# The router of a mixture-of-experts encoder on unscaled rows, and the prompt's list of rows made ahead of the sample's

## Chip, cores and metric

One core of a Trainium2 chip runs the whole kernel. The metric is the device time of one execution in microseconds. Three executions of the kernel before took 2691.74, 2692.01 and 2695.96 us, a median of 2692.01 us.

## What is computed

One layer of a bidirectional encoder is applied to two request groups with the same weights: 1024 tokens of a prompt and 256 of a sample, of 1024 columns. The change lies between the output projection and the first expert:

```python
x = x + concat(yA, yB) @ w_out
h = rms_norm(x, ffn_norm_w)                 # x * rsqrt(mean(x*x) + eps) * w
aff = softmax(h @ w_router)                 # 16 experts
gates, idx = top_k(aff.T, cap)              # each expert takes 128 prompt rows, 32 sample rows
for e in range(16):
    xe = h[idx[e]]
    ye = (silu(xe @ wg[e]) * (xe @ wu[e])) @ wd[e] * gates[e]
    out[idx[e]] += ye
x = x + out
```

The prompt and the sample are routed apart: the threshold of one doesn't depend on tokens of the other.

## The kernel before

Everything is a hand-written program for five queues: TensorE (`pe`), VectorE (`dve`), ScalarE (`act`), GpSimd (`pool`) and the DMA queue of SyncE (`sp`). Each queue runs its instructions in the order written, and the queues meet at semaphores. Float32 products are made of a rounded part (`fp32r`, names with `_h`, lines 734) and two bfloat16 cross products with what the rounding left (`_l`, lines 739 and 740).

**Output projection, tiles t = 0 to 9** of 128 tokens, 0 to 7 the prompt's, 8 and 9 the sample's. `wo_half(t, c)` makes 512 columns: eight rounded products, then sixteen cross products. Two halves lie in one PSUM tile `S[:, t % 2]`. Between them TensorE turns the normed rows of tile t-1 (`h2t`, line 728), turns that tile's router values (`aff`, line 1011), makes the router's partial products in four groups of 32 rows of the PSUM bank G (`router_parts`, line 991), turns the next tile's `yt`, and adds up the four groups (`router`, line 999). The last tile has no tile behind it whose products would cover it: `router(9)` takes sixteen wide instructions (line 1003).

**What VectorE does per tile.** It adds the residual (`x2t`, line 1879), forms the softmax of the tile before (lines 1886 to 1891), runs one or more rounds of the ranking, scales the rows by their rstd and the norm's weight (`h2t`, line 1902), copies the turned rows out of PSUM (`h2T`, line 1909), copies the turned router values to the work tile WK (line 1830), and forms the low parts of the next tile (`yT_l`, line 1824). ScalarE squares `x2t` for the norm (line 1439), GpSimd forms the rstd (lines 2133, 2135) and stores `x2t` (line 2307) and `h2t` (line 2309) to DRAM.

**Ranking.** An expert's 128 greatest of 1024 are found on VectorE in rounds: `MAX8` takes the eight greatest of a row, `MATCH_REPLACE8` takes them out (`best_eight`, lines 1837, 1839). Part 0 (tiles 0 to 3) and part 1 (tiles 4 to 7) take 16 rounds each, on 48 partitions; `merge` (lines 1845 to 1855) merges the halves of a part. The tables `ROUNDS_AHEAD` and `ROUNDS_BEHIND` say at which tile which rounds run, ahead of or behind the middle of VectorE's work. The last four rounds run after the last tile and on 80 partitions, the sample's among them (line 1927).

**Lists.** The threshold is turned by TensorE (line 1031) and compared with `aff` (`chosen`, line 1939); TensorE counts the ranks of the chosen rows (line 1036); VectorE forms places and one-hot rows (`oh` for the prompt, `ohs` for the sample, lines 1944 to 1959); TensorE multiplies them with row numbers and gates (lines 1061, 1064); VectorE adds the parts to indices (`index_sum`, lines 1971 to 1981). GpSimd splits `aff` into three bfloat16 parts for this (`gate_parts`, lines 2291 to 2299), and gathers the rows: `xe`, 128 prompt rows of 4 KB (line 2326), and `xsm`, two gathers of 128 pieces of 512 bytes, the sample's (line 2329).

**First expert.** TensorE turns `xe` and `xsm` (lines 1073, 1075), ScalarE rounds them to X (lines 1464, 1466), VectorE subtracts (lines 1992, 1995), GpSimd converts to bfloat16 (`Xb`, line 2346). Before that VectorE splits weight pieces 0 and 1 (`p_lows`, line 1986). Then 16 experts of 34 weight pieces follow; SyncE loads weights into four stages and waits for the split of a stage's last piece (line 701).

The lines on which the order at the end hangs:

```python
for r in range(r0, r1):                                  # 1835, best_eight
best_eight(1, 80, 12, 16)                                # 1927
onehots(1)                                               # 1999
index_sum(1)
dve.wait_ge(gather_sent, 1)
p_lows(0)
p_lows(1)
```

## Time and profile before

| What | Value |
|---|---|
| median of three executions | 2692.01 us |
| span of the profiled execution, which is its own time here | 2693.8 us |
| TensorE busy | 2606.6 us, 97% |
| VectorE, ScalarE, GpSimd busy | 1963.9, 1692.7, 1108.9 us |
| mean granted TensorE clock | 0.988 of full |
| output projection, all ten tiles | 615.6 to 751.0 us |
| from its last product to the first expert's first product | 751.0 to 793.4 us |
| sixteen experts and the final norm | 793.4 to 2693.8 us |
| GpSimd's constants of the lists, in tile 1 | 646.5 to 654.7 us |
| last index sum of the first expert ends | 781.03 us |

The page gives busy time and share for each engine, then the span in 40 slices; a slice is 67 us, so that the 42 us between the projection and the first expert show as one slice in which TensorE and its clock fall to 6 tenths. The timeline and the tables by stretch show what lies within it. The profile gives no time of its execution outside its span, so the span stands for it; it lies 1.8 us above the median.

### The profile page before, as it was taken

The numbers are of one execution on the slowest core, as the hardware profiler recorded it, in microseconds if no ns is written. First come the engines' busy times: TensorE is split into PE (matmuls) and PEld (weight loads), VectorE is DVE, ScalarE is ACT, GpSimd is POOL, SyncE is SP. The second block draws the span as 40 slices with busy tenths as digits, with TensorE's granted clock in tenths as the row PEclk, the third lists the DMA queues.
The fourth block names the chain that finished last, engine by engine and source line by source line (L and its number), as shares of the span: only waits on it lengthen the run. The fifth ranks groups of instructions, "written<-read, shape, count | busy, mean of one in ns | idle before, by whom it ended". The sixth has DMA issues, their size and how long they took to land. (4 is left out here: it accounts for less than half of the span.)

```text
span 2693.8 us, 53857 instructions
## 1 busy us (share of the span) xinstructions
PE 2606.6 (97%) x22588; PEld 2372.4 (88%) x22588; DVE 1963.9 (73%) x2361; ACT 1692.7 (63%) x2527; POOL 1108.9 (41%) x781
## 2 busy tenths in 40 slices
PE   7999999989959999999999999999999999999997
PEld 6666776665549999999999999999999999999997
DVE  6233256674668788888878888787878878788787
ACT  4366345562127676676767677676766767677675
POOL 2224201134125364452736346263644627354354
PEclk9999999999969999999999999999999999999998
DMA  7311312124557898979889897988988798898887
GB/s 188 76 46 32 74 37 44 36 85 150 168 199 274 314 313 297 330 256 342 293 319 315 292 333 258 340 294 314 322 293 322 269 330 304 311 323 289 317 299 285
DMA packets 365898, 652.18 MB, mean 242 GB/s; under 512 B 26599, under 2 KB 94055, under 8 KB 365623
## 3 DMA queue, kind: packets, MB, share of 16 engines
q1 hardware_dynamic: 349483, 605.63, 64.5%
q0 software_dynamic: 16176, 43.12, 6.3%
q8 instruction: 180, 2.95, 0.5%
q14 instruction: 59, 0.48, 0.1%
HBM read 612.81 MB, written 36.94 MB: 241 GB/s over the span
## 5 line engine op out<-in xcount | busy, mean ns | idle before, releaser
L1986 DVE TENSOR_TENSOR wl<-stg,wh 128x2048 bf16<-128x2048 f32 (+1 forms) x544 | 1241.0, 2289 | 256.6 <-ACT wh L1476 251.8
L1476 ACT ACTIVATE wh<-stg 128x2048 fp32r<-128x2048 f32 (+1 forms) x544 | 1010.9, 1861 | 196.2 <-PE S L1104 71.4
L2379 POOL TENSOR_TENSOR hx<-hh,hx 128x320 fp32r<-128x320 f32 x176 | 385.6, 2191 | 805.9 <-ACT hx L1529 805.6
L1101 PE MATMUL S<-X,wh 128*128 128x320 f32 x3760 | 591.0, 312 | 1.3 <-DVE X L1995 1.3
L1101 PEld LDWEIGHTS S<-X,wh 128*128 128x128 f32 x3760 | 557.1, 189 | 1.7 <-DVE X L1995 1.7
L1147 PE MATMUL S<-hx,wh 128*128 128x320 f32 x1892 | 312.6, 313 | 0.5 <-DVE yTs L2034 0.5
L1101 PE MATMUL OG<-X,wh 128*128 128x320 f32 x1872 | 298.2, 311 | 1.2 <-DVE gg L2016 1.2
L1104 PE MATMUL S<-Xb,wl 128*128 128x160 bf16 x3760 | 290.1, 233 | 0.0
L1147 PEld LDWEIGHTS S<-hx,wh 128*128 128x128 f32 x1892 | 280.8, 188 | 0.9 <-issue 0.6
L1101 PEld LDWEIGHTS OG<-X,wh 128*128 128x128 f32 x1872 | 277.4, 188 | 1.6 <-issue 1.4
L1104 PEld LDWEIGHTS S<-Xb,wl 128*128 128x128 bf16 x3760 | 258.9, 98 | 12.0
L2381 POOL CAST hb<-hx 128x320 bf16<-128x320 f32 x176 | 208.5, 1185 | 0.0
L1529 ACT ACTIVATE hx<-hh 128x320 fp32r<-128x320 f32 x176 | 83.1, 472 | 176.6 <-DVE hh L2023 176.6
L2208 POOL TENSOR_TENSOR ca<-lsum,half 128x20 f32<-128x20 f32 (+3 forms) x10 | 24.2, 2418 | 374.0 <-ACT o_all L1354 236.6
L1104 PE MATMUL S<-hb,wl 128*128 128x160 bf16 x1892 | 158.8, 233 | 0.0
L1147 PE MATMUL OG<-hx,wh 128*128 128x320 f32 x924 | 158.2, 313 | 0.2 <-DVE gg L2016 0.2
L1319 ACT ACTIVATE E<-E,nmax 128x1024 f32<-128x1024 f32 (+1 forms) x80 | 81.8, 1023 | 107.7 <-DVE nmax L1698 107.7
L1104 PE MATMUL OG<-Xb,wl 128*128 128x160 bf16 x1872 | 149.2, 233 | 0.0
L1104 PEld LDWEIGHTS S<-hb,wl 128*128 128x128 bf16 x1892 | 132.1, 98 | 8.1
L1147 PEld LDWEIGHTS OG<-hx,wh 128*128 128x128 f32 x924 | 138.6, 188 | 0.6 <-DVE gg L2016 0.6
L1104 PEld LDWEIGHTS OG<-Xb,wl 128*128 128x128 bf16 x1872 | 129.7, 98 | 6.0
L740 PE MATMUL OG<-hT_h,wkq_l 128*128 128x512 bf16 (+1 forms) x384 | 129.3, 350 | 0.0
(316 smaller groups left out, 3803.5 us busy)
## 6 DMA issues: line engine op xcount, KB each, us to landing
stg<-in_w_gate_dram SPq DMA_DIRECT2D x80, 2048.0 KB
stg<-in_w_up_dram SPq DMA_DIRECT2D x80, 2048.0 KB
stg<-in_w_down_dram SPq DMA_DIRECT2D x64, 2048.0 KB
stg<-in_w_down_dram SPq DMA_DIRECT2D x32, 1536.0 KB
stg<-in_w_gate_dram SPq DMA_DIRECT2D x16, 1024.0 KB
stg<-in_w_up_dram SPq DMA_DIRECT2D x16, 1024.0 KB
w_st<-in_w_in_dram SPq DMA_DIRECT2D x20, 512.0 KB, 4.0
yt<-mixed SPq DMA_DIRECT2D x10, 512.0 KB, 5.4
```

The source lines that it names most:

```text
L740: mm = pe.matmul(out, lhs_l(k), tops(rhs_h(k)), start=False, stop=(k == KT - 1))
L1101: pe.matmul(out, w, x, start=first, stop=False, skip_group_check=True)
L1104: return pe.matmul(out[:, 0:CT], w, x, start=False, stop=last, skip_group_check=True)
L1147: mm = pe.matmul(down_bank(e, d), whk[:, f, c * P:(c + 1) * P], hx[:, f0 + f, :], start=(f0 + f == 0), stop=(last and f0 + f == FT - 1), s ...
L1319: act.activation(e, e, ACT.Exp, scale=-1.0, bias=nmax[:, col:col + 1], accum_out=lsum[:, j % 2, t, hf:hf + 1]).then_inc(exp_done, 1)
L1476: act.activation(piece_conv(wh, g), piece_stage(g), ACT.Copy).then_inc(rounded, 1)
L1529: act.activation(hx[:, j - 1:j + 1, 0:CT], hh[:, :, :], ACT.Copy).then_inc(hidden_hi, 1)
L1986: dve.tensor_tensor(piece_conv(wl, g), piece_stage(g), piece_conv(wh, g).bitcast(F32), ALU.subtract).then_inc(split, 1)
L2208: own(pool.tensor_tensor(a, ls, minus_one, ALU.pow))
L2379: pool.tensor_tensor(hx[:, f, CT:2 * CT], hh[:, :, :], hx[:, f, 0:CT].bitcast(F32), ALU.subtract).then_inc(hidden_ready, 1)
L2381: pool.tensor_copy(hb[:, f, :], hx[:, f, 0:CT].bitcast(F32)).then_inc(hidden_b, 1)
```

## The change

The router's weight is multiplied once with the norm's weight, and the router runs on the unscaled rows `x2t`; the rstd is multiplied onto the logits. TensorE turns `x2t` in the midst of the next tile's products. The last tile takes the four groups too. ScalarE copies the turned rows and scales `h2t`, and GpSimd multiplies the norm's weight on and stores it. The rounds of the ranking are placed anew, the sample's four rounds run on its own 16 partitions after the prompt's threshold, and thresholds, ranks, one-hots, indices and gathers of the first expert are made for the prompt first, then for the sample.

```diff
-ROUNDS_AHEAD = {6: (0, 5, 6), 7: (0, 11, 12), 10: (1, 5, 6)}
-ROUNDS_BEHIND = {5: (0, 0, 5), 6: (0, 6, 11), 7: (0, 12, 16), 9: (1, 0, 5), 10: (1, 6, 11), 11: (1, 11, 12)}
+ROUNDS_AHEAD = {5: (0, 0, 8), 6: (0, 9, 16), 9: (1, 0, 8), 10: (1, 10, 16)}
+ROUNDS_BEHIND = {5: (0, 8, 9), 9: (1, 8, 10)}
...
+                sp.dma_start(fwT[:, :], ffn_norm_w[0].rearrange("(k p) -> p k", p=P)).then_inc(wrt_in, 16)
...
+            def wo_tile(t):
...
+                    highs(S[:, t % 2, cols], y_h(t), o_h(cols), range(KT))
+                    crosses(S[:, t % 2, cols], y_h(t), y_l(t), o_h(cols), o_l(cols), range(4))
+                    rows_turn(t - 1)
+                    crosses(S[:, t % 2, cols], y_h(t), y_l(t), o_h(cols), o_l(cols), range(4, KT))
+                    router_parts(t - 1)
+                cols = slice(512, 1024)
+                highs(S[:, t % 2, cols], y_h(t), o_h(cols), range(KT))
+                if t >= 1:
+                    router(t - 1)
+                if t + 1 < TT:
+                    y_turn(t + 1)
+                crosses(S[:, t % 2, cols], y_h(t), y_l(t), o_h(cols), o_l(cols), range(KT)).then_inc(mixed_ready, 1)
+                if t >= 1:
+                    aff_turn(t - 1)
+
+            def rows_turn(t):
+
+                pe.wait_ge(x2_ready, t + 1)
+                for c in range(2):
+                    turn(wo_fill["h", t] + c, [x2t[:, b * P:(b + 1) * P] for b in range(4 * c, 4 * c + 4)])
...
+            for t in range(TT):
+                wo_tile(t)
+            rows_turn(TT - 1)
+            router_parts(TT - 1)
+            router(TT - 1)
+            aff_turn(TT - 1)
...
+            for u in range(TT - 1):
+                x2_square(u)
+                x2_copies(u)
+                h2_scale(u)
+                parts_copy(u)
+                logit_exp(u)
+                if u + 2 < TT:
+                    y_round(u + 2)
+            x2_copies(TT - 1)
+            x2_square(TT - 1)
+            parts_copy(TT - 1)
+            h2_scale(TT - 1)
+            logit_exp(TT - 1)
...
+            def h2_scale(u):
+                act.wait_ge(rs2_ready, u + 1)
+                if u >= 1:
+                    act.wait_ge(h2_stored, 16 * u)
+                act.activation(h2t[:, :], x2t[:, :], ACT.Copy, scale=rsx[:, TT + u:TT + u + 1]).then_inc(h2_scaled, 1)
...
+            dve.wait_ge(wrt_in, 48)
+            dve.tensor_tensor(wrt[:, :, :], wrt[:, :, :], fwT[:, :].unsqueeze(2).to_broadcast([P, KT, NE]),
+                              ALU.mult).then_inc(wr_ready, 1)
...
+                own(dve.tensor_scalar(lz[:, v % 2, :], G[:, 0:NE], rsx[:, TT + v:TT + v + 1], None, ALU.mult))
...
+            merge(1)
...
+            dve.tensor_copy(least[:, :], cutoff[:, 0:1].to_broadcast([NE, P])).then_inc(cutoff_ready, 1)
+            affT_copy(TT - 1)
+            dve.wait_ge(cutoff_ps, 1)
+            choose(0, TPR, S[:, 0, 0:NE])
+            dve.wait_ge(affT_ready, TT)
+            best_eight(1, slice(64, 80), 0, 4)
+            dve.tensor_copy(least_s[:, :], ranked[64:80, 1, 31:32].to_broadcast([NE, P])).then_inc(cutoff_ready, 1)
...
+            place(0, TPR, ranks)
+            dve.wait_ge(cutoff_ps, 2)
+            choose(TPR, TT, S[:, 1, 0:NE])
...
+            row_onehots(1).then_inc(first_oh, 1)
+            dve.wait_ge(pos_ps, 2)
+            dve.wait_ge(chosen_ready, 2)
+            place(TPR, TT, ranks_s)
+            dve.wait_ge(h2_stored, 16 * TT)
+            piece_onehots(1)
...
-            onehots(1)
-            index_sum(1)
-            dve.wait_ge(gather_sent, 1)
+            dve.wait_ge(first_ps, 1)
+            row_sum(1).then_inc(first_idx, 1)
+            dve.wait_ge(idx_ps, 1)
+            piece_sum(1)
...
             p_lows(0)
             p_lows(1)
-            for q in range(4):
-                x_lows(q + 1, q, q)
             p_lows(2)
             onehots(2)
...
-                pool.wait_ge(h2_ready, t + 1)
+                pool.wait_ge(h2_scaled, t + 1)
+                if t == 0:
+                    pool.wait_ge(wrt_in, 48)
+                own(pool.tensor_tensor(h2t[:, :], h2t[:, :], fwb[:, :], ALU.mult))
+                own.wait()
                 pool.dma_start(octet_of(hn_d, t), h2t[:, :]).then_inc(h2_stored, 16)
...
+            pool.wait_ge(first_idx, 1)
+            stand()
+            gather_rows(1)
+            pool.wait_ge(idx_ready, 1)
+            stand()
+            gather_pieces(1)
```

TensorE waits for `Xb` only ahead of the first low products of an expert (`x_b`, `first_b_s`), no longer ahead of its first rounded ones.

TensorE in one tile of the projection, before: the second half's eight rounded products come after the turned rows and router values; of the runs of cross products (lines 739 and 740) the first two rows stand.

```order
L740 MATMUL S<-wo_h,yT_l 128x512
L728 MATMUL PT<-identf,h2t 128x128 x8
L1011 MATMUL OG<-identf,aff 16x128
L734 MATMUL S<-wo_h,yT_h 128x512 x8
L991 MATMUL OG<-h2T,wrt 16x128 x8
L728 MATMUL PT<-identf,yt_127 128x128 x8
L739 MATMUL S<-wo_l,yT_h 128x512
```

The same place of the change:

```order
L753 MATMUL S<-wo_h,yT_l 128x512
L741 MATMUL PT<-identf,x2t 128x128 x8
L752 MATMUL S<-wo_l,yT_h 128x512
...
L753 MATMUL S<-wo_h,yT_l 128x512
L1029 MATMUL OG<-h2T,wrt 16x128 x8
L747 MATMUL S<-wo_h,yT_h 128x512 x8
L1036 MATMUL OG<-sum_groups,part_logits 128x16
L741 MATMUL PT<-identf,yt_127 128x128 x8
L752 MATMUL S<-wo_l,yT_h 128x512
```

The turned rows moved forward into the first half's cross products, the router's sum from the end of the tile to the middle of its second half, and the turned router values (line 1042) behind the tile.

VectorE from the last tile's softmax to the places, before (`ranked` and WK are the ranking's tiles, `least` the threshold spread over 128 columns):

```order
L1891 TENSOR_SCALAR aff<-eg,rl_118 128x16
...
L1830 COPY WK<-OG 16x128
L1837 MAX ranked<-WK 80x8
L1839 MATCH_REPLACE WK<-ranked,WK 80x256
...
L1934 COPY least<-cutoff 16x128
L1939 TENSOR_TENSOR chosen<-aff,S 128x128 x2
L1939 TENSOR_TENSOR chosen<-aff,S 128x32 x2
L1944 SCALAR_TENSOR_TENSOR places<-chosen,S 128x320
```

and in the change:

```order
L2015 COPY least<-cutoff 16x128
L1911 COPY WK<-OG 16x128
L1999 TENSOR_TENSOR chosen<-aff,S 128x128 x2
L1918 MAX ranked<-WK 16x8
L1920 MATCH_REPLACE WK<-ranked,WK 16x256
...
L2021 COPY least_s<-ranked 16x128
L2004 SCALAR_TENSOR_TENSOR places<-chosen,S 128x2x128
L2007 TENSOR_TENSOR posm<-places 128x8x16
L1999 TENSOR_TENSOR chosen<-aff,S 128x32 x2
L2032 TENSOR_TENSOR oh<-iotaS,posm 128x1024
L2004 SCALAR_TENSOR_TENSOR places<-chosen,S 128x2x32
```

Four rounds moved from ahead of the prompt's threshold to behind it; they stand ahead of the prompt's places and one-hot rows still.

VectorE around the first expert's rows, before (`wl` are the low parts of the weights, X the rows):

```order
L1981 TENSOR_REDUCE gate<-PT 128x1
L1986 TENSOR_TENSOR wl<-stg,wh 128x2048 x2
L1992 TENSOR_TENSOR X<-PT,X 128x4x32
L1995 TENSOR_TENSOR X<-PT,X 128x2x128 x2
L1992 TENSOR_TENSOR X<-OG,X 128x4x32
L1995 TENSOR_TENSOR X<-OG,X 128x2x128 x2
L1986 TENSOR_TENSOR wl<-stg,wh 128x2048
L1956 TENSOR_TENSOR oh<-iotaS,posm 128x1024
```

and in the change, where the two weight pieces stand behind the rows:

```order
L2067 TENSOR_REDUCE gate<-PT 128x1
L2105 TENSOR_TENSOR X<-PT,X 128x2x128 x2
L2105 TENSOR_TENSOR X<-OG,X 128x2x128 x2
L2110 TENSOR_TENSOR X<-S,X 128x4x32 x2
L2086 TENSOR_TENSOR wl<-stg,wh 128x2048 x3
L2032 TENSOR_TENSOR oh<-iotaS,posm 128x1024
```

## Rows read from the trace of the kernel before

**Rows 1.** Table by stretch: start:end, length, busy time of each engine, clock, DMA.

```profile
751.00:793.40 42.40, 11.91 (x82) 10.17 (x82) 28.19 (x88) 10.95 (x18) 13.83 (x21) 0.53 0.33 122
...
912.40:2547.00 1634.60, 1634.58 (x15121) 1608.12 (x15120) 1351.25 (x1244) 1154.91 (x1310) 792.49 (x448) 1.00 0.88 307
```

**Rows 2.** Timeline of TensorE, tiles 3 to 9: start us, length us, engine, line.

```profile
660.70 2.07 PE L734 MATMUL S<-wo_h,yT_h 128*128 128x512 f32 x8
...
687.75 2.09 PE L734 MATMUL S<-wo_h,yT_h 128*128 128x512 f32 x8
...
744.69 2.10 PE L734 MATMUL S<-wo_h,yT_h 128*128 128x512 f32 x8
```

**Rows 3.** Timeline of VectorE behind the last product of the projection.

```profile
751.07 1.23 DVE L1879 TENSOR_TENSOR x2t<-S,xt 128x1024 f32<-128x1024 f32 x1 [0.21 <-PE S L740]
...
763.80 0.23 DVE L1891 TENSOR_SCALAR aff<-eg,rl 128x16 f32<-128x16 f32 x1
...
765.22 0.42 DVE L1837 MAX8 ranked<-WK 80x8 f32<-80x256 f32 x1
...
769.12 0.22 DVE L1928 COPY least<-ranked 16x128 f32<-16x128 f32 x1
...
773.86 0.68 DVE L1939 TENSOR_TENSOR chosen<-aff,S 128x128 bf16<-128x128 f32 x4 [0.43 <-PE S L1031]
777.18 0.49 DVE L1944 SCALAR_TENSOR_TENSOR places<-chosen,S 128x320 f32<-128x320 bf16 x1 [2.64 <-PE S L1036]
...
778.06 1.23 DVE L1956 TENSOR_TENSOR oh<-iotaS,posm 128x1024 bf16<-128x1024 f32 x1
...
780.28 0.22 DVE L1971 TENSOR_SCALAR idx<-PT 128x1 uint32<-128x1 f32 x1 [0.59 <-PE PT L1064]
```

**Rows 4.** Timeline of ScalarE in the same stretch.

```profile
752.48 1.06 ACT L1439 ACTIVATE sq<-x2t 128x1024 f32<-128x1024 f32 x1 [4.79 <-DVEq L1882]
757.81 0.60 ACT L1458 ACTIVATE h2T<-PT 128x512 f32<-128x512 f32 x1 [3.89 <-PE PT L728]
```

**Rows 5.** Timelines of GpSimd and TensorE, first gather to first expert.

```profile
782.04 1.07 POOL L2326 DMA_INDIRECT xe<-ffn_in,idx  x1 [16.04 <-DVE gate L1981]
...
789.74 0.66 PE L1073 MATMUL PT<-identf,xe 128*128 128x128 f32 x2 [9.49 <-DMA xsm<-ffn_in,idx]
...
793.39 7.04 PE L1101 MATMUL S<-X,wh 128*128 128x320 f32 x32 [1.28 <-DVE X L1995]
```

**Rows 6.** Tile view of `xsm`, first expert: min/median/max ns, first and last start.

```profile
L2329 POOL DMA_INDIRECT xsm<-ffn_in,idx x2: 1872/2188/2505, 783.4 to 786.2; - x2
```

**Rows 7.** Timelines of VectorE and GpSimd within an expert, 969 to 974 us.

```profile
970.29 3.65 DVE L1986 TENSOR_TENSOR wl<-stg,wh 128x2048 bf16<-128x2048 f32 x1 [1.13 <-ACT wh L1476]
...
969.92 0.95 POOL L2329 DMA_INDIRECT xsm<-ffn_in,idx  x1 [0.30 <-issue]
970.89 0.90 POOL L2379 TENSOR_TENSOR hx<-hh,hx 128x320 fp32r<-128x320 f32 x1
```

**Rows 8.** Groups by line and shape, GpSimd: count, busy us, mean ns.

```profile
L2379 POOL TENSOR_TENSOR hx<-hh,hx 128x320 fp32r<-128x320 f32 x176 | 385.6, 2191 | 805.9 <-ACT hx L1529 805.6
L2221 POOL TENSOR_TENSOR o_all<-o_all,ca 128x1280 f32<-128x1280 f32 x7 | 18.0, 2565 | 0.5
```

**Rows 9.** Timeline of GpSimd, first and last of the five operations on the gates.

```profile
757.38 0.77 POOL L2291 CAST NG<-aff 128x128 bf16<-128x128 f32 x1
...
760.22 0.75 POOL L2299 CAST NG<-g_rest 128x128 bf16<-128x128 f32 x1
```

**Rows 10.** Tile views of `ffn_in`, `wrt` and `xe`: issue to landing.

```profile
DMA to landing us min/median/max: 4.7/5.0/7.2
...
DMA to landing us min/median/max: 4.1/4.1/4.1
...
DMA to landing us min/median/max: 3.5/5.8/8.0
```

**Rows 11.** Waits from 920 to 2600 us: total us, times, longest.

```profile
ACT wh L1476 <- DMA stg<-in_w_down_dram: 1.9, 2, 1.0
```

More of the change, by code:

```diff
@@ new lines, in y_h, with y_l, o_h, o_l @@
+            def y_h(t):
+                return lambda k: yT_h[:, t % 2, k, :]
+            def y_l(t):
+                return lambda k: yT_l[:, t % 2, k, :]
+            def o_h(cols):
+                return lambda k: wo_h[:, k, cols]
+            def o_l(cols):
+                return lambda k: wo_l[:, k, cols]
+            def wo_tile(t):
+                if t == 0:
+                    pe.wait_ge(scores_read, 2 * STEPS)
+                if t >= 2:
+                    pe.wait_ge(mixed_read, t - 1)
+                pe.wait_ge(turned_copied, wo_fill["y", t] + 2)
+                cols = slice(0, 512)
+                if t == 0:
+                    for m in range(KT // 2):
+                        pe.wait_ge(wo_split, m + 1)
+                        highs(S[:, 0, cols], y_h(0), o_h(cols), (2 * m, 2 * m + 1))
+                        crosses(S[:, 0, cols], y_h(0), y_l(0), o_h(cols), o_l(cols), (2 * m, 2 * m + 1))
+                else:
+                    highs(S[:, t % 2, cols], y_h(t), o_h(cols), range(KT))
[12 more added lines that the diff above has]
+                    aff_turn(t - 1)
@@ new lines, in x2_square, with x2_copies @@
+            def x2_square(u):
+                act.wait_ge(x2_ready, u + 1)
+                if u >= 1:
+                    act.wait_ge(ss2_ready, u)
+                act.activation(sq2[:, :], x2t[:, :], ACT.Square,
+                               accum_out=ssx[:, TT + u:TT + u + 1]).then_inc(ss2_ready, 1)
+            def x2_copies(u):
+                for c in range(2):
+                    f = wo_fill["h", u] + c
+                    act.wait_ge(turned, f + 1)
+                    if u >= 1 and c == 0:
+                        act.wait_ge(parts_ps, u)
+                    act.activation(h2T[:, 4 * c:4 * c + 4, :], PT[:, f % 2, :].rearrange("p (k n) -> p k n", k=4),
+                                   ACT.Copy).then_inc(turned_copied, 1)
@@ new lines, in _ @@
+            y_lows(1)
+            for u in range(TT):
+                t = u + 1
+                dve.wait_ge(mixed_ready, t)
+                dve.wait_ge(xt_in[u % 2], 16 * (u // 2 + 1))
+                if u >= 1:
+                    dve.wait_ge(x2_stored, 16 * u)
+                    dve.wait_ge(h2_scaled, u)
+                    dve.wait_ge(turned, wo_fill["h", u - 1] + 2)
+                own(dve.tensor_tensor(x2t[:, :], S[:, u % 2, :], xt[:, u % 2, :], ALU.add))
+                own.wait()
+                dve.sem_inc(mixed_read, 1)
+                dve.sem_inc(x2_ready, 1)
+                if u >= 1:
+                    affT_copy(u - 1)
+                if t in ROUNDS_AHEAD:
+                    part, r0, r1 = ROUNDS_AHEAD[t]
+                    dve.wait_ge(affT_ready, 4 if part == 0 else TPR)
+                    best_eight(part, slice(0, 48), r0, r1)
+                if t == 7:
+                    merge(0)
+                softmax(u)
@@ L1919, in _, with choose, place @@
                 if t in ROUNDS_BEHIND:
-                    best_eight(part, 48, min(r0 + 2, r1), r1)
-                if t == 8:
-                    merge(0)
-                if t >= TT:
-                    affT_copy(t - 2)
-            dve.wait_ge(affT_ready, TT)
-            best_eight(1, 80, 12, 16)
-            dve.tensor_copy(least[32:48, :], ranked[64:80, 1, P - 1:P].to_broadcast([NE, P]))
+                    part, r0, r1 = ROUNDS_BEHIND[t]
+                    best_eight(part, slice(0, 48), r0, r1)
+            def choose(t0, t1, lim):
+                for m, op in enumerate((ALU.is_gt, ALU.is_equal)):
+                    ins = dve.tensor_tensor(chosen[:, m, t0:t1, :], aff[:, t0:t1, :],
+                                            lim.unsqueeze(1).to_broadcast([P, t1 - t0, NE]), op)
+                ins.then_inc(chosen_ready, 1)
+            def place(t0, t1, counted):
+                own(dve.scalar_tensor_tensor(places[:, :, t0:t1, :], chosen[:, :, t0:t1, :], -10000.0, counted,
+                                             ALU.mult, ALU.add))
+                own.wait()
+                own(dve.tensor_tensor(posm[:, t0:t1, 0:NE], places[:, 0, t0:t1, :], places[:, 1, t0:t1, :], ALU.min))
+                own.wait()
             merge(1)
```

320 lines of the change are left out of this document (144 added, 176 removed).

## Prediction

> **What bounds the kernel now.** I read the 40 slices first, then a table by stretch, then timelines of the one stretch where TensorE stands. The slices show TensorE full but for the start, the end and one slice. In the stretch of 42.4 us between the projection's last product and the first expert TensorE is busy for 11.9 us, at a mean clock of 0.53, while in the experts it is busy for 1634.6 of 1634.6 us at 1.00 [rows 1]. So the experts are bound by TensorE and move as a block: a microsecond saved ahead of them is saved at the end. The stretch itself is one chain: residual, normed rows, router, softmax, rounds, merge, threshold, ranks, one-hots, indices, gathers, turned rows. Most links are VectorE's.
>
> The profiled span is 2693.8 us, 1.8 above the median of 2692.0. The sum is made against the span and taken off the median.
>
> **Stalls in the tiles: 2.8 us gained.** Tiles 3 and 4 took 27.05 us, or 13.53 each. The four periods from 687.75 to 744.69 took 56.94, which is 2.8 more than four such [rows 2]; in them VectorE's rounds delayed `h2t`, for which TensorE waited. The change turns `x2t`. That is ready about 1.5 us into the next tile, and TensorE turns it after eight rounded and eight cross products, at 3.7 us: 2.2 us of cover. TensorE's work per tile is the same otherwise. ScalarE gets two copies (1.2 us) and a scaling (about 1.06, as the square over as many elements) per tile [rows 4], which fit into 13.5 us. The router's sum comes at 9.5 us, softmax follows to about 11.2, and the next tile's low parts are ready at 12.6, so 0.9 us is what covers them. Eight rounds ahead of the softmax (7.8 us at 0.975, since four run from 765.22 to 769.12 [rows 3]) end at 9.7: they just fit. If this cover is gone, TensorE waits for `yT_l`.
>
> GpSimd gets the product with the norm's weight over 1024 columns. It isn't in the trace. A lower bound is 2.1 us, from 2565 ns for 1280 columns; an upper one is 7.0, from 2191 ns for 320 columns beside VectorE's weights [rows 8]. I take 2.4, since VectorE runs rounds then, not splits. It is followed by the store (landing 4.7 to 7.2 [rows 10]), and nothing but the next scaling waits for it: at 2.4 it costs nothing.
>
> **The last chain, after the last product.** In the last tile VectorE has add and copy (1.9), eight rounds (7.8), softmax (1.5) and two more rounds (1.95), or 13.2 us against TensorE's 12.6: the residual starts 0.55 late. From there, ends counted from the last product:
> - residual 1.23 [rows 3] and the copy of tile 8's router values, 0.6: **2.4**;
> - six rounds, 5.85: **8.2**. Beside them run turned rows (1 to 2 us at either clock level), copies (2 x 0.60, overlapped), square 1.06, partial sums and rstd, and scaling 1.06 [rows 4], which end near 8.0: the rounds lead, with little to spare;
> - softmax, about 1.3: **9.5**. Now `aff` ends at 764.03, 13.0 after the product [rows 3];
> - merge and threshold, now 769.34 to 773.43, 4.1: **13.6**; the prompt's threshold no longer waits for four rounds;
> - a delay by GpSimd, below, 2.5: **16.1**;
> - turned threshold 0.43 and two of four comparisons, 0.4: **16.95**;
> - the sample's four rounds and its threshold, 3.9 + 0.2: **21.1**. They cover the prompt's ranks on TensorE (under 2.64 now) but are longer. VectorE is one queue, so the prompt's list still waits for them;
> - prompt's places 0.75, sample's comparisons 0.25, one-hots 1.15: **23.2** [rows 3];
> - sample's places and one-hots 0.95, prompt's index 0.35: **24.5**. So "ahead" is only some 0.6 us;
> - GpSimd's start, now 1.0 after the last index (at 781.03, its gather at 782.04 [rows 5]): **25.5**;
> - `xe` lands 3.5 to 8.0 after its issue [rows 10]; uncontended I take 4.0: **29.5**; eight turns at the lower clock, 1.75: **31.3**. Meanwhile two gathers of `xsm` take 1.0 each instead of 2.5 and 1.87 [rows 6], since VectorE no longer splits weights beside them (0.95 within the expert just before a split begins [rows 7]), and land near 30.6;
> - two sample turns, their rounding and subtraction, 1.5: **32.8**.
>
> Against 42.4 that is 9.6 us less; with the tiles 12.4. A shorter last step is part of it: 3.65 us now from first turn to first product [rows 5], of which ten turns are 2.0.
>
> **GpSimd beside the merge.** Five operations on the gates, 757.38 to 760.97 [rows 9], ran beside rounds. In the change they start behind the last product and its store, near 10.6, beside the merge. Within an expert a split issued at 970.29 took 3.65 us instead of 2.29, while GpSimd's product ran to 971.79 [rows 7]: VectorE stood for 1.4 us. No row shows the merge's small operations beside GpSimd. The bounds are 0 and 3.3 (the sum of the five); I take 2.5, near the upper, as the split's row is the nearest in kind. The Trainium skill, "SBUF — State Buffer", section "SBUF: two separate sides", says the same of any VectorE operation with two SBUF inputs and a GpSimd operation that reads SBUF: whichever starts first holds a shared port pair for its whole length. By that rule the sum would be that of the upper bound, 11.6 us gained; were it not to hold for so small operations, 14.9. The trace agrees for splits.
>
> **Behind the start.** VectorE now splits pieces 0, 1, 2 (2.29 each) and makes one-hots (1.7) after the rows. Pieces 0 and 1 are done 4.6 us after TensorE starts; it needs them after its rounded products, 7.04 us [rows 5]. Hidden, with 2.4 us to spare. Piece 2 ends at 6.9 instead of 2.1, and with it the next load starts 4.8 us later against TensorE; its piece is wanted some 25 us in. ScalarE waited 1.9 us in 1634 for a weight [rows 11], so the lag is taken up. The conversions to bfloat16 are needed at 7 us too. The new transfer `fwT` has 1024 pieces of 4 bytes; `wrt`, 1024 pieces of 64 bytes, landed in 4.1 us [rows 10], and VectorE has some 9 us from issue to `yT_l` of tile 1. Costs nothing unless it lands later.
>
> **Forecast:** 2692.0 - 12.4 = 2679.6, so 2679.5 us.
>
> **Rivals.**
> - *No delay at the merge* (0.2): the chain is 2.5 shorter: 2677. For it: the operations are of 16 partitions and 0.2 us.
> - *The weight stream bounds the first experts* (0.08): then what counts is the load behind piece 2, which starts only 12.4 - 4.8 = 7.6 us earlier: 2684.4. Against it speak rows 11.
> - *The small transfer lands late* (0.07): if 4-byte pieces take three times `wrt`'s 4.1 us, `yT_l` of tile 1 waits some 3.4 us: 2683. The Trainium skill, "DMA: Bandwidth & Descriptors", section Bandwidth, calls transfers under 64 KB dominated by their descriptors; by that alone it would land as `wrt` did, with as many.
> - *The store loop of `h2t` becomes the bound* (0.04): scaling, product, store and the next scaling form a ring, since one buffer serves all tiles. At 7.0 for the product [rows 8] and 7.2 for the landing [rows 10] a turn is 1.06 + 7.0 + 7.2 + 0.55 = 15.8 us against 13.5. ScalarE, standing in `h2_scale`, holds the partial sums, exps and `yT_h`. Eight turns cost 18.2, the constants of the lists (8.2 us on GpSimd in tile 1, longer than the landing that would cover them) some 2 more, and 1.9 are slack: 18.3 lost against 12.4 gained, 2698, slower. It decides once product and landing pass 11.9 us together. Against it: at 2.4 they are under 10.
> - *Less than it says* (0.09): the rounds ahead of the softmax and slower gathers together eat 6 to 8 us, 2686 to 2688; the prompt's head start of 0.6 us wouldn't show at all, as the rows then wait for the pieces.
>
> **How the numbers follow.** The forecast has 0.52. Its own bounds: merge 0 to 3.3, landing 3.5 to 8, gathers 1.0 to 2.2 each. Executions of this kernel differ by 4 us, and 0.2%, or 5.4 us, is about what a measurement can tell from no change. The range 2674 to 2687 takes in the first three rivals and leaves out about 2 in 10. Faster by over 5.4 us (under 2686.6): 0.52 + 0.2 + 0.08 + 0.06 + little of the rest, 0.87; within 0.2%: 0.08; slower: 0.05, the ring and what I have not seen.
>
> **What would show it.** Tiles of 13.5 us throughout; `x2t` turned without a wait; the stretch without TensorE near 33 us; the merge stretched from 3.3 to 5 or 6 beside GpSimd's five operations; `xsm` issued in about 1 us each; TensorE without a wait between its first rounded and low products. Wrong it would be if tiles grew past 14 us, if a wait for `h2_stored` stood on ScalarE, or if the stretch were over 37 us.

## The result, and the profile after

| | before | changed |
|---|---|---|
| median of five executions | 2695.96 us (2691.74 to 2696.75) | 2680.64 us (2679.00 to 2683.25) |
| profiled execution: time, span | 2695.96, 2693.8 us | 2681.98, 2680.2 us |
| ratio | | 0.9947, 95% interval 0.9936 to 0.9957 |

The change is faster, by 15.3 us between the medians and 14.0 between the profiled executions. The forecast was 2679.5 us, the range 2674 to 2687.

Line numbers from here on are those of the changed kernel; in an edited kernel they are its own, a few lines off. The table by stretch answers to [rows 1]: start:end, length, busy time and instructions of TensorE, its weight loads, VectorE, ScalarE, GpSimd, then clock, share of the DMA engines, GB/s.

```profile
748.50:780.90 32.40, 8.84 (x85) 6.68 (x84) 24.09 (x82) 11.70 (x18) 14.11 (x23) 0.59 0.53 198
780.90:787.60 6.70, 6.68 (x35) 6.60 (x36) 6.70 (x4) 1.20 (x1) 0.00 (x0) 0.71 0.01 2
899.90:2534.50 1634.60, 1634.52 (x15122) 1608.22 (x15121) 1350.84 (x1244) 1154.27 (x1310) 791.90 (x448) 1.00 0.88 307
```

The stretch between the projection's last product and the first expert is 32.4 us long instead of 42.4. Behind it TensorE is as full as before. The last product's end moved too, from 750.98 to 748.52 us. So the first expert starts 12.5 us earlier: 2.5 from the tiles, 10.0 from the stretch.

TensorE's timeline in the tiles answers to [rows 2]. The rows of line 747 are the first products of the second halves of four tiles, the row of line 741 is a turned residual.

```profile
688.53 2.14 PE L747 MATMUL S<-wo_h,yT_h 128*128 128x512 f32 x8
...
702.11 2.11 PE L747 MATMUL S<-wo_h,yT_h 128*128 128x512 f32 x8
...
712.36 1.03 PE L741 MATMUL PT<-identf,x2t 128*128 128x128 f32 x8
...
715.64 2.11 PE L747 MATMUL S<-wo_h,yT_h 128*128 128x512 f32 x8
...
742.72 2.14 PE L747 MATMUL S<-wo_h,yT_h 128*128 128x512 f32 x8
```

The halves are 13.53 to 13.58 us apart from tile to tile, also where rounds run, and the residual is turned without a wait. The four periods that took 56.94 us take 54.19 (688.53 to 742.72), 2.75 less.

The last chain on VectorE, with what answers to [rows 3]:

```profile
748.61 1.22 DVE L1978 TENSOR_TENSOR x2t<-S,xt 128x1024 f32<-128x1024 f32 x1
...
756.19 0.23 DVE L1959 TENSOR_SCALAR lz<-OG,rsx 128x16 f32<-128x16 f32 x1
756.46 0.95 DVE L1961 CUSTOM_DVE_ANT_0 lg<-lz,zer 128x16 f32<-128x16 f32 x1
...
758.08 0.97 DVE L1966 TENSOR_SCALAR aff<-eg,rl 128x16 f32<-128x16 f32 x1
759.09 0.22 DVE L1926 COPY merges<-ranked 16x128 f32<-16x128 f32 x1
759.34 0.49 DVE L1928 TENSOR_TENSOR merges<-ranked,merges 16x128 f32<-16x128 f32 x1
...
763.61 0.21 DVE L2015 COPY least<-cutoff 16x128 f32<-16x128 f32 x1
...
764.21 0.48 DVE L1999 TENSOR_TENSOR chosen<-aff,S 128x128 bf16<-128x128 f32 x2
...
768.59 0.21 DVE L2021 COPY least_s<-ranked 16x128 f32<-16x128 f32 x1
768.83 0.42 DVE L2004 SCALAR_TENSOR_TENSOR places<-chosen,S 128x256 f32<-128x256 bf16 x1
...
771.84 0.22 DVE L2059 TENSOR_SCALAR idx<-PT 128x1 uint32<-128x1 f32 x1
```

From the residual to the index VectorE hardly stands: it is one queue, and it is the chain. Two entries are odd. `lg` and `aff` take 0.95 and 0.97 us; in a tile where GpSimd is idle they take 0.17 and 0.23. GpSimd's timeline shows what ran beside them, and the gathers:

```profile
755.04 2.33 POOL L2420 TENSOR_TENSOR h2t<-h2t,fwb 128x1024 f32<-128x1024 f32 x1 [0.68 <-ACT h2t L1508]
...
758.26 0.76 POOL L2400 CAST NG<-aff 128x128 bf16<-128x128 f32 x1
759.11 0.57 POOL L2402 TENSOR_TENSOR g_rest<-aff,NG 128x128 f32<-128x128 f32 x1
...
773.12 1.07 POOL L2437 DMA_INDIRECT xe<-ffn_in,idx  x1 [9.11 <-DVE gate L2067]
774.50 0.98 POOL L2443 DMA_INDIRECT xsm<-ffn_in,idx  x1 [0.30 <-issue]
775.78 0.96 POOL L2443 DMA_INDIRECT xsm<-ffn_in,idx  x1 [0.30 <-issue]
```

`lg` ends as the product does (757.37), `aff` as the cast does (759.02). In this profile `aff` starts 0.18 us ahead of that cast, so that the profile alone doesn't say which held which; the first run below does. The second and third gather are issued in 0.98 and 0.96 us where [rows 6] has 1.87 and 2.51. TensorE then waits for the rows, not for the pieces as in [rows 5]:

```profile
777.61 1.08 PE L1140 MATMUL PT<-identf,xe 128*128 128x128 f32 x4 [5.42 <-DMA xe<-ffn_in,idx]
...
779.34 0.63 PE L1144 MATMUL S<-identf,xsm 128*128 128x128 f32 x2
780.92 6.66 PE L1150 MATMUL S<-X,wh 128*128 128x320 f32 x32 [0.95 <-DVE X L2105]
787.42 2.39 PE L1153 MATMUL S<-Xb,wl 128*128 128x160 bf16 x32
```

The low products follow the rounded ones without a gap, so the splits that now come last are hidden.

### The profile page after: what moved, and what is told of

It reads as the page before. It is cut to its first block and busy times, and to the rows that moved or that the text cites. A ratio compares the mean times of both kernels' runs of the same rounds, so it can differ in the third digit from the quotient of the medians.

```text
span 2680.2 us, 53857 instructions
## 1 busy us (share of the span) xinstructions
PE 2599.1 (97%) x22537; PEld 2368.6 (88%) x22592; DVE 1950.2 (73%) x2357; ACT 1712.2 (64%) x2556; POOL 1127.7 (42%) x792
```

## The experiments

All are edits of the changed kernel. Executions of one kernel differ by some 5 us, more than most of these edits are worth, so I read them in their profiles, by the time from the end of the projection's last product to the first expert. It is 32.40, 32.49 and 32.40 us in three profiles of the changed kernel. The expectations count from the forecast's 32.8 where they name an absolute time; what is compared below is the difference. One execution each of the first seven edits took 2680.3 to 2686.6 us.

**GpSimd's gate operations out of the chain.** The prompt's five are issued in tile 7:

```diff
                 if t == 1:
                     list_constants()
+                if t == TPR - 1:
+                    pool.wait_ge(aff_ready, TPR)
...
+                    gate_parts(0, TPR)
...
-            for t0, t1 in ((0, TPR), (TPR, TT)):
-                pool.wait_ge(aff_ready, t1)
...
-                gate_parts(t0, t1)
+            pool.wait_ge(aff_ready, TT)
...
+            gate_parts(TPR, TT)
```

> The change, with GpSimd's five operations on the prompt's gates moved from behind the last tile's store to behind tile 7's (its affinities are there by then). Only the sample's five small ones (0.3 us each) are left beside the merge. My theory (GpSimd holds VectorE's operations in the last chain): the product with the norm's weight, 2.33 us, stays where it is and still stretches the softmax's first subtraction (0.95 instead of 0.17 us); the last step of the softmax, `aff`, goes from 0.97 back to 0.23, and merge and threshold from 4.7 to 4.1 to 4.4 us. The first expert starts 1.0 to 1.3 us earlier, 31.4 to 31.8 us behind the last product's end instead of 32.8. Rival (no delay by GpSimd, the long entries belong to VectorE itself or to its waits): `aff` stays at 0.97, merge at 4.7, and the start moves by under 0.2 us.

Measured: 31.08 us, 1.32 less. `aff` is back at 0.23, and from its end to the threshold's end it is 4.23 us instead of 4.77; `lg` stays at 0.97 beside the product. So GpSimd's operations on the gates held `aff` and the merge. VectorE's timeline of this run:

```profile
757.24 0.97 DVE L1961 CUSTOM_DVE_ANT_0 lg<-lz,zer 128x16 f32<-128x16 f32 x1
...
758.88 0.23 DVE L1966 TENSOR_SCALAR aff<-eg,rl 128x16 f32<-128x16 f32 x1
```

**And the last product behind the threshold.**

```diff
+                if t == TT - 1:
+                    pool.wait_ge(cutoff_ready, 1)
                 own(pool.tensor_tensor(h2t[:, :], h2t[:, :], fwb[:, :], ALU.mult))
```

> As early_parts, and GpSimd's product for the last tile waits for the prompt's threshold, so that it runs beside the sample's rounds; the sample's gate operations follow it. My theory: none of softmax, merge and threshold is stretched any more: first subtraction 0.17, `aff` 0.23, merge and threshold 4.1 us; in sum 2.0 to 2.2 us less than in the change, the first expert 30.5 to 30.9 us behind the last product's end. The product's store is issued at some 18.5 us and lands 3.6 to 4 later, just before the lists need it (23), so it costs nothing; if it lands 7.9 us behind its issue, as the slowest did, the gather is late by up to 3. The rounds (MAX8 0.42, MATCH_REPLACE8 0.40) are not stretched, as they weren't beside the products of the tiles before. Rival (a GpSimd operation only slows what runs beside it, whatever it is): the rounds, places or one-hots take up what the merge no longer does, and the start is where early_parts has it.

Measured: 30.22 us, 2.18 less than the change. Nothing on VectorE is stretched; the threshold is ready at 13.15 us behind the last product instead of 15.30. The product now runs beside `chosen` and the rounds, and neither gets longer. GpSimd's delay in the chain is therefore worth 2.15 us: 0.78 at `lg`, 0.74 at `aff`, the rest, 0.64, in the merge. What becomes of this gain at the end of the program stands with the last runs below. VectorE's timeline:

```profile
757.03 0.17 DVE L1961 CUSTOM_DVE_ANT_0 lg<-lz,zer 128x16 f32<-128x16 f32 x1
...
757.88 0.23 DVE L1966 TENSOR_SCALAR aff<-eg,rl 128x16 f32<-128x16 f32 x1
```

**The sample's rounds back ahead of the merge.**

```diff
+            affT_copy(TT - 1)
+            dve.wait_ge(affT_ready, TT)
+            best_eight(1, slice(64, 80), 0, 4)
             merge(1)
...
-            affT_copy(TT - 1)
             dve.wait_ge(cutoff_ps, 1)
             choose(0, TPR, S[:, 0, 0:NE])
-            dve.wait_ge(affT_ready, TT)
-            best_eight(1, slice(64, 80), 0, 4)
```

> The change with the sample's four rounds put back ahead of the merge, as the kernel before has them (without the threshold's copy). My theory (the rounds cover the prompt's counts on TensorE, and VectorE is one queue): 3.9 us of rounds move ahead of the merge; behind the comparisons VectorE then waits some 2.4 us for the counts, in which the sample's threshold and comparisons (0.5) fit. So the chain would be 2.1 to 2.4 us longer, less 0.6 that the merge no longer loses beside GpSimd's operations, as they end under the rounds: 1.5 to 1.9 us later start of the first expert, 34.3 to 34.7 us behind the last product. Rival (the order itself is what the change gains, and the prompt's list is ahead by the rounds' full length): 3.9 us later, 36.7. Rival (nothing but the sum of VectorE's work counts, since the sample's list comes last in any case): within 0.5 us of the change.

Measured: 34.73 us, 2.33 more. VectorE's timeline has the wait that came back, and one I had left out, 0.47 us for the turned router values of the last tile:

```profile
759.99 0.28 DVE L1911 COPY WK<-OG 16x128 f32<-16x128 f32 x1 [0.47 <-PE OG L1042]
...
764.50 0.28 DVE L1928 TENSOR_TENSOR merges<-ranked,merges 16x128 f32<-16x128 f32 x1
...
771.69 0.42 DVE L2004 SCALAR_TENSOR_TENSOR places<-chosen,S 128x256 f32<-128x256 bf16 x1 [2.25 <-PE S L1055]
```

The order is worth the 2.25 us of TensorE's counts that the rounds cover, not the rounds' 3.9. With the wait that I had left out it comes to more than the 1.5 to 1.9 that I expected.

**The splits back ahead of the rows.** `p_lows(0)` and `p_lows(1)` stand behind the index again, ahead of the subtractions.

> The change with VectorE's splits of the weight pieces 0 and 1 (2.29 us each alone) put back ahead of the subtractions of the turned rows, that is, beside the three gathers. My theory (a split holds GpSimd while it makes a gather's descriptors): the gathers, issued in 1.07, 0.98 and 0.96 us in the change, take 1.9 to 2.5 us each for those that meet a split, two or three of them; the rows land 0.9 to 1.4 us later and the pieces 2 to 3 us later, and the first expert starts 1.5 to 2.5 us later, 34.3 to 35.3 us behind the last product. Behind the start nothing is gained, as TensorE finds both pieces ready either way. Rival (the gathers got shorter for another reason: the tile, the lists or the emptier queue): issues stay at about 1 us each and the start within 0.3 us of the change.

Measured: 34.11 us, 1.71 more. GpSimd's timeline, then VectorE's:

```profile
773.62 2.79 POOL L2437 DMA_INDIRECT xe<-ffn_in,idx  x1 [9.11 <-DVE gate L2067]
776.72 1.81 POOL L2443 DMA_INDIRECT xsm<-ffn_in,idx  x1 [0.30 <-issue]
778.83 0.96 POOL L2443 DMA_INDIRECT xsm<-ffn_in,idx  x1 [0.30 <-issue]
```

```profile
773.18 4.48 DVE L2086 TENSOR_TENSOR wl<-stg,wh 128x2048 bf16<-128x2048 f32 x2
```

The first gather ends 0.94 us behind the end of the first split (4.48 for two, so some 775.4), the second 0.9 behind that of the second, as if each got going only once a split is done. TensorE's first turn of `xe` comes 1.71 us later than in the change, so the whole loss comes by the rows' gather. VectorE's two splits are as short as alone. The Trainium skill, "SBUF — State Buffer", section "Who interferes with whom", lets a VectorE operation with two SBUF inputs hold only GpSimd's reads and infers that the making of descriptors isn't held by one. For these gathers the trace disagrees: 2.79 and 1.81 us against 0.96 to 1.07. They also read their indices from SBUF (`idx` in the rows); which part of a gather the split holds, no run separates.

**Both lists awaited before the first gather.** GpSimd waits for `idx_ready` ahead of `gather_rows(1)`.

> The change, but GpSimd waits for both index lists before it issues the prompt's gather, as before the change. My theory (the two lists are only 0.6 us apart, since VectorE makes them in one queue behind the sample's rounds): the gather of the rows is issued 0.5 to 0.7 us later, at 25.5 to 25.7 us behind the last product instead of 25.0, and the first expert starts 0.4 to 0.7 us later. Rival (the head start of the rows carries the gain, by hiding a gather): 1.5 us or more later.

Measured: the gather is issued at 25.29 us instead of 24.60, and the expert starts at 33.10, 0.70 later. The head start is what VectorE's queue leaves of it.

**The prompt's list really ahead.**

```diff
-            best_eight(1, slice(64, 80), 0, 4)
-            dve.tensor_copy(least_s[:, :], ...).then_inc(cutoff_ready, 1)
+            best_eight(1, slice(64, 80), 0, 3)
             dve.wait_ge(pos_ps, 1)
             place(0, TPR, ranks)
...
             row_onehots(1).then_inc(first_oh, 1)
+            best_eight(1, slice(64, 80), 3, 4)
+            dve.tensor_copy(least_s[:, :], ...).then_inc(cutoff_ready, 1)
```

The sum of the prompt's index and the sample's comparisons follow, in this order.

> The change with the prompt's list really ahead: VectorE makes three of the sample's four rounds while TensorE counts, then the prompt's places, one-hots and index, and only then the last round and the sample's threshold; TensorE's products for the prompt's list stand ahead of the sample's counts. My theory (both lists are a queue on VectorE; what the rows gain the pieces lose): the rows' gather starts about 1 us earlier, the pieces' gathers 0.8 to 1.2 us later, and the two sample turns, which need the pieces, begin when they did: start of the first expert within 0.4 us of the change's 32.8. Rival (the chain hangs on the rows, as the change's profile has TensorE waiting for `xe` for 5.4 us): the start comes the full 1 us earlier.

Measured: 31.26 us, 1.14 less; my theory missed, and the rival has it. The rows' gather starts at 23.53 instead of 24.60. The pieces' index is ready 0.97 later, but their gathers start at 26.03 and 27.31 instead of 25.98 and 27.26, only 0.05 later where I had 0.8 to 1.2. GpSimd's timeline:

```profile
771.67 1.07 POOL L2440 DMA_INDIRECT xe<-ffn_in,idx  x1 [8.03 <-DVE gate L2053]
774.17 0.98 POOL L2446 DMA_INDIRECT xsm<-ffn_in,idx  x1 [1.44 <-DVE gate L2072]
775.45 0.96 POOL L2446 DMA_INDIRECT xsm<-ffn_in,idx  x1 [0.31 <-issue]
```

In the change the pieces' index lay ready while GpSimd still issued the rows' gather. That slack pays for the swap.

**The old places of the first rounds.**

```diff
-ROUNDS_AHEAD = {5: (0, 0, 8), 6: (0, 9, 16), 9: (1, 0, 8), 10: (1, 10, 16)}
-ROUNDS_BEHIND = {5: (0, 8, 9), 9: (1, 8, 10)}
+ROUNDS_AHEAD = {6: (0, 5, 6), 7: (0, 11, 12), 9: (1, 0, 8), 10: (1, 10, 16)}
+ROUNDS_BEHIND = {5: (0, 0, 5), 6: (0, 6, 11), 7: (0, 12, 16), 9: (1, 8, 10)}
```

> The change with the old places of the prompt's first set of rounds: five behind tile 4's and 5's low parts and four behind tile 6's, one each ahead of the softmax, and its merge one tile later; the second set stays as changed. My theory (the tables and the turned residual belong together): five rounds behind the low parts end 4.9 us after them and make the residual 3.1 us late; TensorE turns it 3.7 us into the tile, which covers 2.2, so it waits about 1.0 us in each of two tiles and hardly in a third; the last product ends 2.0 to 2.4 us later than in the change, periods of 14.5 instead of 13.53 in those two. The last chain is as in the change, 32.8 us. Rival (turning `x2t` within the next tile's products hides the rounds wherever they stand): all periods stay 13.53. Rival (as before the change, every late us is lost): 3 us in each of two tiles and 2 in the third, 8 us in all.

Measured: the four periods take 56.29 us (689.49 to 745.78) instead of 54.19, 2.10 more, in two tiles; the last chain is 32.35. TensorE's timeline:

```profile
689.49 2.14 PE L747 MATMUL S<-wo_h,yT_h 128*128 128x512 f32 x8
...
700.66 1.09 PE L741 MATMUL PT<-identf,x2t 128*128 128x128 f32 x8 [0.72 <-DVEq L1981]
...
704.00 2.14 PE L747 MATMUL S<-wo_h,yT_h 128*128 128x512 f32 x8
...
715.24 1.09 PE L741 MATMUL PT<-identf,x2t 128*128 128x128 f32 x8 [0.79 <-DVEq L1981]
```

The cover works as expected: the first late residual starts 3.0 us behind its tile's last product (699.22 against 696.20), and 1.0 is lost. But in the two tiles with the old places nothing is gained over the kernel before: their periods take 29.10 us, 29.12 there. The four periods are 0.65 us shorter than before because of the last of them, where the second set of rounds stands at its new places (13.57 us, 14.27 before). So the new places are needed: rounds ahead of the softmax, where VectorE otherwise waits for the logits. Whether they would do without the turned residual isn't shown, as no run turns `h2t` with the new places.

**Four products on GpSimd per tile.** Three more, into a buffer that nothing reads:

```diff
+                for _ in range(3 if t < TT - 1 else 0):
+                    own(pool.tensor_tensor(spare[:, :], h2t[:, :], fwb[:, :], ALU.mult))
+                    own.wait()
                 own(pool.tensor_tensor(h2t[:, :], h2t[:, :], fwb[:, :], ALU.mult))
```

> The change with three more products of the same size on GpSimd in tiles 0 to 8, into a buffer that nothing reads: 9.75 us instead of 2.38 between ScalarE's scaling and the store. It tests the rival of the ring (scaling 1.15, product, store and landing about 4.1, then the next scaling of the one buffer). Mine: one product leaves the ring at some 8.7 us of the tile's 13.53 and is free; with four it is 15.2 us, so periods grow by 1.6 us each once the slack is used, and the list's constants (8.2 us on GpSimd in tile 1) delay the next rstd by up to 7 once: the last product 15 to 20 us later, ScalarE standing for `h2_stored` or rstd. The last tile has one product, and the chain behind it stays 32.8 us. Rival (GpSimd has so much idle time that even four are hidden): no tile over 13.6 us. Rival (VectorE's work is held by the products, beside which its residual, low parts and rounds run): growth of several us per tile with long entries on VectorE, more than 20 us in all.

Measured: the last product ends at 782.81 us, some 34 us later than in the change, where I expected 15 to 20, and the kernel takes 2716.91 us, slower than before the change. Two rows of the waits in the tiles (total, times, longest), one of the tile view of `h2t`, and groups of VectorE by line (count, busy us, mean ns):

```profile
ACT h2t L1509 <- DMA ffn_in<-h2t: 24.3, 6, 5.4
...
ACT h2t L1509 <- POOL rsx L2245: 10.9, 2, 8.1
```

```profile
DMA to landing us min/median/max: 3.1/5.3/7.3
```

```profile
L1967 DVE TENSOR_SCALAR aff<-eg,rl 128x16 f32<-128x16 f32 x9 | 15.9, 1770 | 0.3
L1962 DVE CUSTOM_DVE_ANT_0 lg<-lz,zer 128x16 f32<-128x16 f32 x9 | 13.2, 1464 | 0.3
...
L1927 DVE COPY merges<-ranked 16x128 f32<-16x128 f32 x1 | 2.1, 2104 | 0.0
```

The ring of one buffer does bound the tiles then: residuals follow each other after 14.7 to 18.9 us, once, where the list's constants come between, after 22.9. The waits for the store and for the rstd are those I had named. Two sizes were off: the store lands in 5.3 us at the median, not 4.1, and in each tile VectorE is also held for some 2.8 us by the products, at `lg` and `aff`, which stand ahead of the low parts in VectorE's queue. The third view, that the products hold VectorE's work, has the size (more than 20 us) and the engine, but not the operations: residuals, low parts and rounds weren't held. How much of the 34 us is the ring's and how much the hold's wasn't separated.

**All that helped, together.** The three helpful edits; the rounds' last `MATCH_REPLACE8`, whose result is read by nothing, left out; and two copies moved to ScalarE:

```diff
                     own(dve.max(eight, WK[rows, part, :]))
                     own.wait()
+                    if r + 1 == (16 if rows.start == 0 else 4):
+                        break
...
+            act.wait_ge(aff_ps, TT)
+            act.activation(WK[64:80, 1, P:2 * P], O[0:NE, 256:256 + P], ACT.Copy).then_inc(affT_ready, 1)
+            act.wait_ge(ranked_s, 1)
+            act.activation(least_s[:, :], ranked[64:80, 1, 31:32].to_broadcast([NE, P]), ACT.Copy).then_inc(cutoff_ready, 1)
```

> All that helped, together: GpSimd's gate operations behind tile 7 and its last product behind the threshold; the prompt's list ahead of the sample's fourth round; and, new, the last MATCH_REPLACE8 of the prompt's and of the sample's rounds left out (its result is read by nothing), and the copy of the last tile's router values and the sample's threshold copied by ScalarE instead of VectorE. My theory (the last chain is VectorE's queue, and each us taken out of it or no longer held comes off the start): from the change's 32.4 us behind the last product 2.2 for GpSimd, 1.1 for the list, 0.5 for the prompt's replace, 0.3 for the copy, and 0.5 to 0.7 for the sample's, which sets when the pieces' gathers start: 27.7 to 28.3 us. The limit on the other side is the product's store: issued at about 15.5 us, it has to land before the gather at about 20.6; had it the 7.9 us of the slowest store, the gather would wait 3 us. The time: 4.1 to 4.7 us under the change's, a ratio to the kernel before of 0.9930 to 0.9935. Rival (once the rows are early, the chain hangs on the pieces, and what is saved on the prompt's side is lost): 29.5 us.

> The change itself, unaltered, on the chip on which the next kernel runs. Its first expert starts 32.4 us behind the end of the last product; from the first expert's third piece to the last expert's twelfth the profile should be the same to 0.1 us, and what differs from the first profile should be the start of the program (under 1 us) and the last expert's end, where the profiles so far differ by up to 3.6 us. Against the kernel before: 0.995, as measured, with an interval of about 0.001 to either side.

Measured: 28.30 us from last product to first expert, the upper edge of what I expected, against 32.49 in the change's profile of the same chip. The times didn't show the 4.1 to 4.7 us, nor a ratio of 0.9930 to 0.9935: medians 2682.05 and 2682.44 us, ratios to before 0.9952 (0.9938 to 0.9965) and 0.9947 (0.9934 to 0.9961). So both ran again.

> The change once more, beside combined_2, since the last comparison left open whether the 4.2 us that the combined kernel's profile shows are there in the times (medians 2682.4 and 2682.1, each of five executions that scatter over 7 us). If they are, the change's ten executions stand some 4 us above the combined kernel's ten. Chain 32.4 to 32.5 us again.

> The combined kernel unaltered. My theory (what is gained ahead of the experts stays gained, and the last comparison was scatter from the program's start and the last expert): first expert 28.3 us behind the last product, and a median 2 to 5 us below the change's of the same call. Rival (something behind the start gives the gain back in most executions, but not in the one profiled): a median within 1 us of the change's, and a profile in which the stretch from the first expert's third piece to the end is longer by some 3 us than in the change's.

Measured: 28.32 and 32.40 us; medians 2679.31 and 2682.89, ratios 0.9941 (0.9927 to 0.9955) and 0.9956 (0.9942 to 0.9969). Over ten executions each, the combined kernel's mean is 2680.4 us and the change's 2682.4, a difference of 2.0 with a 95% uncertainty of 2.0. That it is faster than before is shown, that it beats the change is likely. From the last product's end to the 41st of ScalarE's 176 Silu operations it is 439.7 and 440.2 us with the combined kernel, 443.3 to 444.1 with the change, and from the 41st to the 171st 1395.0 and 1395.1 against 1394.8 to 1395.0. So the gain of the chain lasts until the last expert. At the very end half of it is given back: GpSimd's scatter of the last expert's prompt rows starts later behind its last operation. GpSimd's timeline in the change, then in the combined kernel:

```profile
2671.04 1.10 POOL L2537 DMA_INDIRECT out_dram<-xe,idx  x1 [2.11 <-issue]
```

```profile
2665.94 1.10 POOL L2551 DMA_INDIRECT out_dram<-xe,idx  x1 [4.27 <-issue]
```

It is 4.27, 4.26 and 4.27 us in `combined`, `combined_2` and `gpsimd_late`, the three profiles in which the last product waits for the threshold, and 2.11 or 2.12 in all eleven others, the kernel before among them. So that edit gains 0.86 us in the chain over `early_parts` and goes with 2.15 lost at the end, and 4.1 less 2.15 is about the 2.0 of the means. Why the scatter starts later stays open: the profile names no releaser, and no run changes it alone. The combined kernel without that edit wasn't run.

**Where executions differ.** The last product of the change ended at 748.5, 749.9 and 749.6 us in three profiles of the same kernel, and at 745.6 and 749.1 in two of the combined kernel. The 745.6 belongs to that kernel's fastest execution, 2676.87 us. In the last expert there is a second such place. The waits of ScalarE around it, in the change and in the run with both lists awaited:

```profile
ACT wh L1551 <- DMA stg<-in_w_up_dram: 3.9, 1, 3.9
```

```profile
ACT wh L1551 <- DMA stg<-in_w_up_dram: 1.4, 1, 1.4
```

One load lands late there. TensorE doesn't feel 1.4 us, and stands 1 to 2 us for 3.9 to 4.6. From the 171st Silu to the last it is 34.8 us in the runs with the short wait and 35.6 to 38.5 in the others, the kernel before among them. `early_parts` shows why this matters: its chain is 1.3 us shorter, and its time, 2683.94 us, is 2 us longer than the change's profiled one, as its last product ended 0.8 later, 0.7 was lost up to the 41st Silu and 2.0 in its last expert.

## Why the prediction was right

The kernel is faster by 14.0 us in the profiled pair where I had 12.4 (15.3 between the medians), and the time falls inside the range. That it lies only 1.1 us from the forecast is luck: the median that I started from was 4 us low, and the gain is 3 us larger. Step by step:

- **Tiles, 2.8:** 2.75 over the four periods. The last product is only 2.46 earlier, since in the new order a second half starts 0.8 us later in its tile and the last tile's is 0.5 shorter. The mechanism holds in its parts: the run with the old rounds loses 2.10, where the same sum gave 2.0 to 2.4, so the new places are needed; and in it 2.0 of 3.0 us of lateness are covered. That the cover is needed beside the new places was argued, and no run takes it away.
- **The product on GpSimd, 2.4:** 2.38 us in each tile, hidden. The ring stays far from the tile's length. The run with four products shows that the rival's ring is real; its 18 us were for one product of 7.0, so that run's 34 us, with 9.75, can't be held against them.
- **The stretch, 9.6:** 10.0. Ends behind the last product, forecast and measured: copy 2.4, 1.8; rounds 8.2, 7.6; threshold with GpSimd's delay 16.1, 15.3; comparisons 16.95, 16.2; sample's rounds 21.1, 20.3; one-hots 23.2, 22.5; index 24.5, 23.6; gather 25.5, 24.6; rows landed 29.5, 29.0; sample turns 31.3, 30.8; first expert 32.8, 32.4. The residual wasn't late: I had put it 0.55 us behind the product, and it starts 0.09 behind, as before the change. The landing took 4.4 instead of 4.0.
- **GpSimd beside VectorE, 2.5:** 2.15 by the run that takes it away. Its size was near in part by luck, and its place was right only in part. I had put all of it at the merge and on the five gate operations; 1.5 of it is in the softmax, 0.78 under the product, which I had not thought of there. Taking the prompt's five away brings 1.32, half of the 2.5, and the merge itself lost only 0.64 beside them, far from the upper bound of 3.3: being issued side by side is not being held for the whole length. The operation `aff` has one tensor as input and was held none the less; [rows 7] showed only a split with two. The Trainium skill, "SBUF — State Buffer", section "Who interferes with whom", counts such a scalar operation and a copy, from SBUF to SBUF, among those that can take the shared ports alone; the trace agrees, with 0.97 us for `aff` against 0.23, and with 2.10 for the merge's copy in the run with four products against 0.22.
- **Gathers at 1.0:** 0.98 and 0.96, and the splits are the cause, by the run that puts them back.
- **Sample's rounds cover the ranks, head start 0.6:** both hold (2.25 us covered; 0.70 for the head start). What I had wrong is the expectation for `rows_sooner`: that with a list further ahead the start would wait for the pieces. It need not, up to about 1 us.
- **Behind the start:** nothing was lost. The wait for `fwT`, which landed in 3.6 us, didn't arise.

The difference left, 14.0 against 12.5 at the first expert, lies behind the start and outside the span. The rounded products of the first piece took 6.66 us instead of 7.04, but at the 41st Silu nothing of that is left (0.03). 0.4 is in the experts' middle, 0.7 in the last expert and the end, where executions of one kernel differ by more. The time outside the span is 1.8 us instead of 2.2. That last pair also corrects a sentence of mine: the profiled execution took 2695.96 us, so its span was not above its time. The median of three that I took the sum off was a low one; executions of the kernel before that ran beside the experiments have medians of 2695.1 and 2695.4. The range held because it was wider than this.

## What to carry to other kernels

Where one engine's queue is the chain, count what another engine's moved work will meet there, operation by operation: GpSimd's operations cost nothing beside `MAX8` and `MATCH_REPLACE8` or beside reads of PSUM, but beside short operations between SBUF tiles from a fifth of their length (the merge's 0.64 us beside 3.4 us of small operations) to most of it (a copy's 1.9 beside a product of 2.4). Issue gathers where VectorE has no split to do, and fill a wait for TensorE with work that something later needs. For edits worth less than the scatter of executions, measure from one event of the profile to the next and not the time, but do so up to the last instruction: the delayed product gained in the chain and lost more behind the last expert. And say so when the time doesn't confirm it.

## What was unexpected of the hardware

- A gather's issue beside a split of weights lasts until 0.9 us behind the split's end (2.79 and 1.81 us), alone 0.96 to 1.07 us. The split isn't slowed.
- A `TENSOR_SCALAR` and a `COPY` with one SBUF tensor as input were held by GpSimd's product (1.77 us at the mean, 2.10); rounds over 256 elements never were (0.42 and 0.40).
- The same first 32 rounded products took 6.2 to 7.5 us over the runs, at a mean clock of 0.71 in the stretch shown above; so executions can differ by up to 1.3 us there.
- 1024 pieces of 4 bytes landed in 3.6 us, no later than 1024 of 64 bytes [rows 10].
